# Hybrid encoder trunk: output projection begun between the second spectra and the inverse transform, spectral sums on VectorE, another order of the last norms, x read back in halves

## The reference

```python
def encoder_layer(x, lp):
    x = x + 0.5 * swiglu(rms_norm(x, lp['norm_ffn1']), lp['ffn1_w_in'], lp['ffn1_w_out'])
    h = rms_norm(x, lp['norm_mix'])
    proj = h @ lp['w_in']
    pa, pb, pc = jnp.split(proj, [A_COLS, A_COLS + B_COLS], axis=-1)
    ya = rwkv7_mixer(pa, lp)
    yb = group_rms_norm(neighbourhood_attention(pb, lp['na_rpb']), lp['na_out_norm'], B_HEADS)
    yc = group_rms_norm(hyena_mixer(pc, lp), lp['hy_out_norm'], C_GROUPS)
    mixed = jnp.concatenate([ya, yb, yc], axis=-1).astype(x.dtype)
    x = x + mixed @ lp['w_out']
    x = x + 0.5 * swiglu(rms_norm(x, lp['norm_ffn2']), lp['ffn2_w_in'], lp['ffn2_w_out'])
    return x
...
def hyena_mixer(p, lp):
    ...
    z = x1 * (fft_long_conv(v, kern_fft[:, 0], seq_len) + v * d_skip[0])
    return x2 * (fft_long_conv(z, kern_fft[:, 1], seq_len) + z * d_skip[1])
```

## Time and profile before

| | |
|---|---|
| median of 3 runs | 3674.84 us (3670.18 to 3675.35) |
| profiled execution | 3673.93 us |
| its span | 3672.1 us |
| PE busy | 3507.9 us (96%) |
| DVE busy | 1806.4 us (49%) |
| ACT busy | 956.9 us (26%) |
| POOL busy | 85.7 us (2%) |
| mean granted TensorE clock | 0.984 |

### The profile page before, as it was taken

The page is one execution under the profiler, slowest core; times in us unless marked ns, Lnnn a source line. Parts: engine busy times, 40 slices in busy tenths (PEclk is TensorE's granted clock), DMA queues, the critical chain, the costliest instruction groups (busy, mean ns, idle before and its releaser), DMA issues.

```text
span 3672.1 us, 60660 instructions
## 1 busy us (share of the span) xinstructions
PE 3507.9 (96%) x26620; PEld 3322.1 (90%) x26620; DVE 1806.4 (49%) x3040; ACT 956.9 (26%) x1511; POOL 85.7 (2%) x86
## 2 busy tenths in 40 slices
PE   7999999999996899999999999999999869999997
PEld 6999999888875899999999999998888649999997
DVE  5443445644677443333453534466366664333334
ACT  3221223112344321211331212232132523211212
POOL 0000000000001000000000100000000010000000
PEclk9999999999998999999999999999999989999998
DMA  3122123230041212222122222132200512122121
GB/s 132 60 75 80 49 69 102 70 118 19 11 152 61 92 57 70 61 63 70 58 75 68 82 69 64 59 105 83 103 3 20 202 40 64 59 68 66 54 71 57
DMA packets 75943, 264.30 MB, mean 72 GB/s; under 512 B 8402, under 2 KB 8402, under 8 KB 73504
## 3 DMA queue, kind: packets, MB, share of 16 engines
q1 hardware_dynamic: 72128, 248.08, 20.4%
q0 software_dynamic: 3552, 12.34, 1.1%
HBM read 230.50 MB, written 29.88 MB: 71 GB/s over the span
## 4 chain that ended last, share of the span: by engine, by line
PE 90%; DVE 6%; issue 1%; ACT 1%; POOL 0%; DMA 0%; DVEq 0%; SPq 0%; POOLq 0%
PE ps L739 90%; DVE uv L2172 1%; PE ps L1219 0%; DVE rstd L1721 0%; DVE sc L2226 0%; DMA x<-xT 0%; DVE hl L1729 0%; DVE NR L1957 0%; POOL sums L729 0%; DVE yab L2180 0%; ACT mh L1650 0%; ACT L1440 0%; DVE xab L2166 0%; DVE xab L2167 0%; PE ps L1139 0%
## 5 line engine op out<-in xcount | busy, mean ns | idle before, releaser
L739 PE MATMUL ps<-hh,wh 128*128 128x384 f32 (+2 forms) x3520 | 1186.9, 337 | 24.5 <-DVE wl L1711 23.4
L739 PE MATMUL ps<-hl,wh 128*128 128x384 f32 (+2 forms) x3520 | 1178.7, 335 | 0.0
L739 PE MATMUL ps<-hh,wl 128*128 128x384 f32 (+2 forms) x3520 | 1178.1, 335 | 0.0
L739 PEld LDWEIGHTS ps<-hh,wh 128*128 128x128 f32 x3520 | 662.8, 188 | 47.0 <-issue 29.5
L739 PEld LDWEIGHTS ps<-hl,wh 128*128 128x128 f32 x3520 | 662.8, 188 | 15.1
L739 PEld LDWEIGHTS ps<-hh,wl 128*128 128x128 f32 x3520 | 662.7, 188 | 14.2
L1356 ACT CAST wh<-wring 128x1024 fp32r<-128x1024 f32 (+2 forms) x372 | 345.9, 954 | 675.1 <-PE ps L739 657.2
L739 PE MATMUL ps<-act_high,wl 128*128 128x384 f32 x1408 | 470.3, 334 | 0.0
L739 PE MATMUL ps<-act_high,wh 128*128 128x384 f32 x1408 | 470.3, 334 | 0.0
L739 PE MATMUL ps<-act_low,wh 128*128 128x384 f32 x1408 | 470.3, 334 | 0.0
L1835 DVE TENSOR_TENSOR silu<-ps,rstd 128x384 f32<-128x384 f32 x176 | 98.0, 557 | 698.8 <-PE ps L739 698.8
(11 more groups left out here) (264 smaller groups left out, 3517.8 us busy)
## 6 DMA issues: line engine op xcount, KB each, us to landing
wring<-wa SPq DMA_DIRECT2D x244, 512.0 KB, 3.6
wring<-wa SPq DMA_DIRECT2D x64, 384.0 KB, 3.2
wring<-wa SPq DMA_DIRECT2D x64, 320.0 KB, 3.0
bias<-bias SPq DMA_DIRECT2D x24, 512.0 KB, 6.8
conv_q_k<-stage SPq DMA_DIRECT2D x28, 384.0 KB, 2.6
kern_rows<-kst POOLq DMA_DIRECT2D x12, 512.0 KB, 4.0
outT<-x SPq DMA_DIRECT2D x2, 3072.0 KB, 10.2
kern<-kern_rows SPq DMA_DIRECT2D x2, 3072.0 KB, 12.4
```

What stands on the lines that cost most here:

```text
L739: return pe.matmul(out, lhsT, rhs, start=start, stop=stop)
```

## The change

- The three spectral sums of each convolution leave POOL; DVE makes them in the fold loop, two instructions of 512 behind `yab`, and `yab` itself is two instructions of 2x256 in place of four of 256. The kernel spectra `kern` are six tensors of 512 KB, loaded by six transfers in place of one.
- The first inverse takes its token tiles in the order 4, 5, 0, 1, 2, 3, and DVE puts its norms, RWKV tile 1 and the low part of tile 0 between the products.
- In the second spectra ACT splits two weight tiles of the projection, and DVE splits them and makes the low parts of k-tiles 2, 3, 1 ahead of the last fold's multiplication. The high part of tile 1 is the last of its four on ACT.
- PE runs the first four k-tiles (0, 2, 3, 1) of units 0 to 3 of the projection between the second spectra and the second inverse, k-tiles 4 and 5 between the last norms, and 6 and 7 in `mix_out`; their sums stay in banks 0 to 3. `gnorm` alternates between banks 6, 7 and 4, 5.
- For the last norms ACT squares both tiles before it takes either root.
- `x` comes back in two halves of 1.5 MB: one after the last second spectrum, one after the last inverse. The ring slots of the second layer's projection are shifted by two.

```diff
+INVERSE_ORDER = (4, 5, 0, 1, 2, 3)
+K_ORDER = (0, 2, 3, 1, 4, 5, 6, 7)
+EARLY_UNITS = 4
...
-        kern = nc.alloc_sbuf_tensor_at("kern", [P, 3, 2, 2, 512], F32, offset=LATE)
-        assert LATE + 24576 <= Z_MIXED
+        KERN_AT = [(8192, 12288, 26624), (0, 4096, 16384)]
+        kern = [[nc.alloc_sbuf_tensor_at(f"kern{o}{a}", [P, 2, 2, 256], F32, offset=LATE + KERN_AT[o][a]) for a in range(3)]
+                for o in range(2)]
...
+        def slot_of(n):
+
+            shift = 0
+            for l in L:
+                if n >= use_base(l, 2):
+                    shift = (2 - use_base(l, 2)) % SPLITS
+            return (n + shift) % SPLITS
...
-                        sp.dma_start(kern[:, :, :, :, :].rearrange("p a k t c -> p a (k t c)"),
-                                     kern_d[l].rearrange("a p k c -> p a (k c)")).then_inc(s_kl, 16)
+                        for o in range(2):
+                            for a in FOLD_ORDER:
+                                sp.dma_start(kern[o][a][:, :, :, :].rearrange("p k t c -> p (k t c)"), kern_d[l, o, a])\
+                                    .then_inc(s_kl, 16)
...
-                sp.wait_ge(*hp.at(l, "inv", 1, 1))
-                sp.dma_start(x[:, :, :], outT).then_inc(s_back, 16)
+                for i, done in enumerate([("dft", 1, FOLD_ORDER[-1]), ("inv", 1, 1)]):
+                    sp.wait_ge(*hp.at(l, *done))
+                    sp.dma_start(x[:, 4 * i:4 * i + 4, :], outT[:, 4 * i:4 * i + 4, :]).then_inc(s_back[i], 16)
...
-                for o in range(2):
-                    for j, a in enumerate(FOLD_ORDER):
-                        pool.wait_ge(*hv.at(l, "dft", o, a))
-                        ya, yb = yab[:, j % 2, 0, :], yab[:, j % 2, 1, :]
-                        pool.tensor_tensor(sums[:, a, 0, :], ya, yb, ALU.add)
-                        pool.tensor_tensor(sums[:, a, 1, :], ya, yb, ALU.subtract).then_inc(*hq.inc(l, "sums", o, a))
...
             def gnorm():
                 pe.wait_ge(s_g1, gns[0] + 1)
-                if gns[0]:
-                    pe.wait_ge(s_g3, gns[0])
+                if gns[0] > 1:
+                    pe.wait_ge(s_g3, gns[0] - 1)
                 for f in range(2):
-                    m = mm(bank(6 + f, HALF), cs("blk"), sqb[:, gns[0] % 2, f * HALF:(f + 1) * HALF])
+                    m = mm(bank(6 - 2 * (gns[0] % 2) + f, HALF), cs("blk"), sqb[:, gns[0] % 2, f * HALF:(f + 1) * HALF])
                 m.then_inc(s_g2, 1)
...
+                        if o == 1 and j == 1:
+                            pe.wait_ge(*hv.at(l, "inv", 0, INVERSE_ORDER[-1]))
...
-                        for tt in range(6):
-                            if tt >= 2:
-                                pe.wait_ge(*hv.at(l, "inv", 0, tt - 2))
+                        for n, tt in enumerate(INVERSE_ORDER):
+                            if n >= 2:
+                                pe.wait_ge(*hv.at(l, "inv", 0, INVERSE_ORDER[n - 2]))
+                            else:
+                                pe.wait_ge(s_g3, 6 * l + 2)
...
-                        pe.wait_ge(*hv.at(l, "inv", 0, 5))
+                        pe.wait_ge(*hv.at(l, "inv", 0, INVERSE_ORDER[1]))
                     else:
+                        pe.wait_ge(*hv.at(l, "take", 1, FOLD_ORDER[-1]))
+                        for v in range(EARLY_UNITS):
+                            out_unit(l, v, range(0, 4))
+                        pe.wait_ge(s_g3, 6 * l + 4)
...
-                for i in range(2):
-                    gnorm()
+                gnorm()
+                for v in range(2):
+                    out_unit(l, v, range(4, 6))
+                pe.wait_ge(*hv.at(l, "inv", 1, 1))
+                gnorm()
+                for v in range(2, EARLY_UNITS):
+                    out_unit(l, v, range(4, 6))
+
+            def out_unit(l, v, places):
+
+                m_, f = divmod(v, 2)
+                w = tile_in(use_base(l, 2) + m_)
+                cols = slice(f * HALF, (f + 1) * HALF)
+                for p in places:
+                    k = K_ORDER[p]
+                    if v == 0:
+                        pe.wait_ge(s_m, 8 * l + p + 1)
+                    m = mm3(bank(v % 4, HALF), w_k(w, k), (mh[:, k, cols], ml[:, k, cols]), p == 0, p == OUT_TILES - 1)
+                return m
...
-                for m_ in range(OUT_TILES):
-                    w = tile_in(use_base(l, 2) + m_)
-                    for f in range(2):
-                        v = 2 * m_ + f
-                        if v >= 4:
-                            pe.wait_ge(s_xup, x_count(l, 2) + v - 3)
-                        cols = slice(f * HALF, (f + 1) * HALF)
-                        for k in range(OUT_TILES):
-                            if v == 0:
-                                pe.wait_ge(s_m, 8 * l + k + 1)
-                            m = mm3(bank(v % 4, HALF), w_k(w, k), (mh[:, k, cols], ml[:, k, cols]), k == 0, k == 7)
-                        m.then_inc(s_fo, 1)
+                for v in range(2 * OUT_TILES):
+                    if v >= 4:
+                        pe.wait_ge(s_xup, x_count(l, 2) + v - 3)
+                    out_unit(l, v, range(6, 8) if v < EARLY_UNITS else range(8)).then_inc(s_fo, 1)
...
+                        if o and j:
+                            split_to(use_base(l, 2) + j - 1)
                     for i in range(2):
                         gn_root(6 * l + 2 * o + i)
                     if o == 0:
                         for i in range(2):
                             gn(4 + i)
-                        for i in range(2):
-                            sa.wait_ge(*rv.at(l, "done", i))
-                            high_mixed(i)
+                        sa.wait_ge(*rv.at(l, "done", 0))
+                        high_mixed(0)
                         for i in range(2, 4):
                             sa.wait_ge(s_g4, 6 * l + i - 1)
                             high_mixed(i)
+                        sa.wait_ge(*rv.at(l, "done", 1))
+                        high_mixed(1)
                     else:
-                        sa.wait_ge(*hv.at(l, "dft", 1, FOLD_ORDER[-1]))
-                        split_to(use_base(l, 2))
                         for i in range(4, 6):
                             sa.wait_ge(s_g4, 6 * l + i - 1)
                             high_mixed(i)
                 for i in range(2):
                     sa.wait_ge(*hv.at(l, "inv", 1, i))
                     gn(6 + i)
+                for i in range(2):
                     gn_root(6 * l + 4 + i)
...
+                        if o and j == 2:
+                            split_to(use_base(l, 2))
+                            for p in range(1, 4):
+                                low_mixed(l, p)
+                            split_to(use_base(l, 2) + 1)
                         ve.wait_ge(*hv.at(l, "take", o, a))
                         for k in range(2):
                             for trig in range(2):
-                                by = kern[:, a, k, trig, kcol].unsqueeze(1).broadcast_to([P, 2, 256])
+                                by = kern[o][a][:, k, trig, :].unsqueeze(1).broadcast_to([P, 2, 256])
                                 m = TT(uv[:, k, trig, :].rearrange("p (e c) -> p e c", e=2),
                                        xab[:, k, :].rearrange("p (e c) -> p e c", e=2), by, M)
                         step(m)
-                        if j == 2:
-                            ve.wait_ge(*hq.at(l, "sums", o, FOLD_ORDER[0]))
-                        for k in range(2):
-                            y, u, v = yab[:, j % 2, k, :], uv[:, k, 0, :], uv[:, k, 1, :]
-                            TT(y[:, 0:256], u[:, 0:256], v[:, 256:512], SU)
-                            m = TT(y[:, 256:512], u[:, 256:512], v[:, 0:256], AD)
-                        m.then_inc(*hv.inc(l, "dft", o, a))
+                        TT(yab[:, :, 0:256], uv[:, :, 0, 0:256], uv[:, :, 1, 256:512], SU)
+                        TT(yab[:, :, 256:512], uv[:, :, 0, 256:512], uv[:, :, 1, 0:256], AD).then_inc(*hv.inc(l, "dft", o, a))
                         ve.wait_ge(*hv.at(l, "dft", o, a))
+                        TT(sums[:, a, 0, :], yab[:, 0, :], yab[:, 1, :], AD)
+                        TT(sums[:, a, 1, :], yab[:, 0, :], yab[:, 1, :], SU).then_inc(*hq.inc(l, "sums", o, a))
                     if o == 0:
                         tail_end(l, 0)
+                        for n, tt in enumerate(INVERSE_ORDER):
+                            ve.wait_ge(*hp.at(l, "inv", 0, tt))
+                            TT(vx[:, tt, 0, :], vx[:, tt, 1, :], ps[:, 4 + n % 2, 0:256], M).then_inc(*hv.inc(l, "inv", 0, tt))
+                            if n in (1, 2):
+                                gn(1 + n, "na_out_norm", n - 1)
+                            if n == 3:
+                                tail_end(l, 1)
+                            if n == 4:
+                                low_mixed(l, 0)
+                    else:
```

(24 more changed lines are left out.)

45 lines of the change are left out of this document (26 added, 19 removed).

## The result

The changed kernel takes 3638.93 us (median of 4 runs, 3637.42 to 3639.14), the one before 3674.43 beside it. The ratio is 0.9904, 95% interval 0.989 to 0.9917, so it is faster by 35 us, 1%. The forecast of 3642 is 3 us above it, inside the range of 3630 to 3656. The profiled execution took 3639.14 us, its span is 3637.3. The changed kernel, measured again later, gave 3639.33.

What follows compares the result with a forecast made beforehand. The prediction took PE, busy 96% of the span, as the bound, with time to win only where PE waits. It summed 15.8 us a layer, 31.6 in both, from 3673.93 to 3642.3, said as 3642, range 3630 to 3656.

Steps and rivals of the forecast that it cites:

- Sums on DVE: First spectra's fold loop: fold period 6.33 us for 5.32, three folds 19.0 for 18.1, sums ending at 1151.8 against 1154.14.
- First inverse: Convolutions' first inverse: 16 remaining products take 10 us, to 1164.3; DVE starts second spectra's `xab` at 1166.75, 3.7 earlier.
- Early units: PE before the second inverse: operands at 1181.9, full clock from 1188, 48 matmuls end at 1192.8, 1.9 after the sums.
- Last norms: Behind the second inverse: last low part ends at 1214.9 instead of 1222.58, 11.6 us behind the inverse instead of 18.0.
- Rest of the projection: PE behind the last low part: 309 matmuls left instead of 363, 53.6 us instead of 62.9, ending at 1270.
- The 1.5 for half clock: Allowance of 1.5 us added to the projection's remaining matmuls, since PE idles some 4 us ahead of them.
- Edits costed at nothing: x in halves, kernel spectra in six transfers, ring slots: no gain; a late fourth weight tile costs up to 2 us a layer.
- The sum: Whole kernel: 15.8 us a layer, 31.6 in both, taking the profiled 3673.93 to 3642.3.
- rival 1: PE stays at half clock in the early units: 8 to 9 us a layer, time 3659; chance 0.11.
- Rival 3: PE never below full clock from 1182 on: 3.4 us a layer more gain, time 3635; chance 0.04.
- Rivals 2 and 4: 2: last norms don't shorten, 3655, chance 0.11; 4: half clock lasts until low parts are there, 3682, chance 0.02.

## Why the prediction was right

The stage went as written, step by step, in the table above; the worst step of the first layer is off by 0.4 us. Point by point:

- *Sums on DVE*: period 6.40 for 6.33, three folds 19.2 for 19.0, `uv` 2.50. What the move is worth by itself isn't told from nothing. That POOL's share was the cause of the 1.07 was an inference from two rows; the kernel with the sums on POOL has it back.
- *First inverse*: 12.46 us from its first wait's end to the next `xab`, for 12.5. That it fits so well is partly luck: it was worked out from a first inverse with a late rise of the clock, and this profile has the late rise in the first layer. In the second layer the same step took 11.1, and in the first of the kernel measured again 11.3.
- *Early units*: first operands 49.33 for 49.1, half clock until +54.8 for +55.2, end 60.24 for 60.0. One detail was wrong: the first four k-tiles weren't paced by DVE's low parts. PE needed 0.96 for three matmuls at half clock, DVE 0.9 for a low part, and the units went through without a gap. And half clock was priced at twice 0.173 for a matmul (1198.5 for all 48); the trace has 0.32.
- *Last norms*: 11.1 us behind the inverse for 11.6. The step's sum was right, but its words name the averages' half clock and one round trip. Of the 6.9 us won, the order of the roots is 1.0, and the half clock of the averages 2.0. The largest part, 3.9, the prediction doesn't name: ACT's first square no longer waits behind a tile that DVE scales late. It is there already in the kernel with everything undone.
- *Rest of the projection*: 55.5 and 55.3 from the last low part to the last addition's start, for 55.1. The 1.5 for half clock is 1.6 and 1.3 against the 53.9 of the kernel with both last gaps filled.
- *Edits costed at nothing*: x in halves, 0.2 us by the medians and 0.1 by the stages, so nothing that can be told. The ring slots and the six transfers weren't tried by themselves.
- *The sum*: 31.6 forecast, 35 measured, and both layers' stages 34.6. What was mis-sized is the second layer, which I set equal to the first. It gained 18.74, 2.9 more. The split between the layers is chance in part (when measured again, the first gains 17.7 and the second 16.4), the sum isn't. Of the 2.9, 1.6 is the kernel before, which had 64.87 us behind its last low part there, for 63.28 in the first layer. At the last low part the changed kernel is 2.0 sooner in the second layer than in the first (below), the one before 0.9, which makes 1.1; the rest, 0.2, is behind it.
- *Rivals*: the half clock did come as in rival 1, but for 17 of 48 matmuls only. Rival 3, all of it at the full clock, was priced at 3.4 a layer; the unread matmuls that brought it about for the early units gave 1.4 there, of which 0.57 reached the last addition. Rivals 2 and 4 didn't occur.

So 27 of the 35 us are shown by taking the parts away, over half of them the early units. The other 8 are read from the traces: no run isolates the scaling, the joined `yab`, the six transfers or the ring slots. The split of the 27 among the small parts stays open, since the executions of one kernel lie 1 to 7 us apart. Least certain are the sums, 0 to 2.6, and the inverse's order, 2.8 or 4.5.

## What to carry to other kernels

Work of a stage that is bound by PE, put into a wait of PE in the stage ahead, gives its whole time if its operands come from an engine that has room; count then what it delays (here 2.1 us at the start of the inverse and 0.9 in the last norms) against what it spares, which includes the half clock of the work behind the wait (2.1). Where an in-order engine holds a cheap piece that waits for something late in front of the first link of a chain, moving this piece seems to have won more (5.9 us up to the last low part, 2.0 of clock included; read from two traces, not shown by a run of its own) than the order of the chain's links (1.0). In this dense stage the gaps of 2 to 6 us that remained cost twice, as gap and as half clock behind it; unread matmuls in them gave 7 to 9 of the 13 us that were still to be had.

## What the runs showed of the hardware

A standstill of PE of 1.9 us behind another of 1.7, with three matmuls between, was enough for the granted clock to fall to 0.5 for the next 3.4 to 6.2 us, and matmuls at 0.17 us in both gaps were enough to keep it at 1.0. The prediction put 1.5 us a layer on this as given; unread matmuls gave all of it back.

The moment at which the clock falls and rises wasn't fixed by the program alone. The first inverse of the changed kernel, the same 32 matmuls, in the first and in the second layer, PE in order of time:

```profile
1155.65 10.08 PE L753 MATMUL ps<-sums,gtab 128*128 128x256 f32 x32 [8.30 <-DVE vx L2223]
```

```profile
2950.36 8.74 PE L753 MATMUL ps<-sums,gtab 128*128 128x256 f32 x32 [6.71 <-DVE vx L2223]
```

In the sooner case the eight matmuls ahead of the idle time ran at half clock (3.58 us, in the other 1.99). The clock by windows:

```profile
1160.00:1162.00 2.00, 2.00 (x7) 1.60 (x6) 0.82 (x1) 1.15 (x2) 0.00 (x0) 0.61 0.00 0
...
2953.00:2955.00 2.00, 2.00 (x9) 1.68 (x8) 1.04 (x2) 0.00 (x0) 0.00 (x0) 0.86 0.00 0
```

By the mean clock of these windows it rises 5.9 us after the start of these matmuls in one (0.22 of the first window at the full clock) and 3.2 us in the other (0.72 of the second). The 2.7 us between, at half clock, are the 1.34 us between the two rows. When the changed kernel was measured again, the sooner one was in the first layer (`xab` at +32.89) and the later one in the second (+34.12). So 1.3 us of a stage, and 2 us at its last low part (+80.08 and +81.88), are chance of the execution. In both executions one layer had the sooner rise and one the later, and the two layers' sum moved by 0.5 us only. A difference of 1 to 2 us between two kernels in one layer needs more than one profile.
